# Delta heads of a hybrid decoder step: normalisation moved from keys and queries to factors per token

## The reference, cut to what matters

```
qkv_a  = h @ w_in[...];  conv = causal depthwise convolution of width 4 of q, k, v;  silu
qa = l2_normalize(qa) * HEAD_DIM_A ** -0.5
ka = l2_normalize(ka)              # x * rsqrt(sum(x*x) + 1e-6)
G = cumsum(log_a);  decay[i,j] = exp(G_i - G_j), i >= j
a_mat = strict lower part of (beta_i k_i . k_j) * decay
solve (I + a_mat) [w, u] = [beta k exp(G), beta v]
v_new = u - w S;   o = (q exp(G)) S + ((q . k) * decay) v_new
S = S * exp(G_last) + (k exp(G_last - G))^T v_new
o_a = rms_norm(o, gnorm_a) * silu(z)
```

## Time and profile before

| | us |
|---|---|
| median of 3 runs | 1989.44 (1988.54 to 1991.89) |
| the profiled execution's own time | 1989.23 |
| its span | 1987.2 |
| PE busy | 1910.3 (96% of the span) |
| DVE busy | 755.8 (38%) |
| ACT busy | 619.8 (31%) |
| POOL busy | 559.3 (28%) |

### The profile page before, as it was taken

The page is one execution under the profiler, slowest core; times in us unless marked ns, Lnnn a source line. Parts: engine busy times, 40 slices in busy tenths (PEclk is TensorE's granted clock), DMA queues, the critical chain, the costliest instruction groups (busy, mean ns, idle before and its releaser), DMA issues.

```text
span 1987.2 us, 29633 instructions
## 1 busy us (share of the span) xinstructions
PE 1910.3 (96%) x12298; PEld 1855.4 (93%) x12298; DVE 755.8 (38%) x1525; ACT 619.8 (31%) x1335; POOL 559.3 (28%) x332
## 2 busy tenths in 40 slices
PE   6899999999999999999989999999999999999998
PEld 6898998999999899988989999999999999999997
DVE  5552552552452312332346424641252145115413
ACT  5532342342342323334424323321231023103311
POOL 1241141131131110211114434531343234214431
PEclk9999999989999999999989999999999999999999
DMA  5312312312312432444554332221121122112212
GB/s 155 87 52 62 98 51 59 102 46 64 94 53 86 143 105 94 148 132 145 181 171 146 98 87 75 84 65 43 53 90 49 43 66 84 43 53 74 64 53 88
DMA packets 235839, 173.25 MB, mean 87 GB/s; under 512 B 16277, under 2 KB 225250, under 8 KB 235322
## 3 DMA queue, kind: packets, MB, share of 16 engines
q1 hardware_dynamic: 200586, 131.57, 22.4%
q10 hardware_dynamic: 35120, 39.80, 6.1%
HBM read 134.04 MB, written 47.72 MB: 91 GB/s over the span
## 4 chain that ended last, share of the span: by engine, by line
PE 81%; DVE 8%; ACT 4%; DMA 4%; issue 2%; POOL 1%; SPq 0%; DVEq 0%; ACTq 0%; POOLq 0%
PE dense L207 50%; PE dense L232 13%; PE work L1359 1%; PE work L1371 1%; PE work L995 1%; PE work L1005 1%; DVE systems L853 1%; PE work L1409 1%; PE work L207 1%; PE work L1392 1%; PE work L1351 1%; PE work L935 1%; PE work L1003 1%; PE work L962 1%; PE work L410 1%
## 5 line engine op out<-in xcount | busy, mean ns | idle before, releaser
L196 POOL TENSOR_TENSOR WL<-Wraw,WH 128x1024 fp32r<-128x1024 f32 (+1 forms) x131 | 315.3, 2407 | 1075.2 <-ACT WH L191 1075.1
L207 PE MATMUL dense<-hH,WH 128*128 128x352 f32 x1392 | 456.0, 328 | 5.5 <-POOL WL L196 5.5
L207 PE MATMUL dense<-hL,WH 128*128 128x352 f32 x1392 | 450.7, 324 | 0.0
L207 PE MATMUL dense<-hH,WL 128*128 128x352 f32 x1392 | 450.3, 324 | 0.0
L232 PE MATMUL dense<-hH,WH 128*128 128x352 f32 x744 | 268.8, 361 | 5.6 <-ACT fill L241 5.3
L207 PEld LDWEIGHTS dense<-hH,WH 128*128 128x128 f32 x1392 | 265.0, 190 | 6.9 <-POOL WL L196 5.7
L207 PEld LDWEIGHTS dense<-hL,WH 128*128 128x128 f32 x1392 | 265.1, 190 | 0.0
L207 PEld LDWEIGHTS dense<-hH,WL 128*128 128x128 f32 x1392 | 264.6, 190 | 0.0
L207 PE MATMUL dense<-gH,WH 128*128 128x352 f32 x768 | 247.5, 322 | 2.5 <-DVE gL L1754 1.7
L191 ACT ACTIVATE WH<-Wraw 128x1024 fp32r<-128x1024 f32 (+1 forms) x131 | 136.3, 1041 | 363.7 <-PE dense L207 296.3
L207 PE MATMUL dense<-gL,WH 128*128 128x352 f32 x768 | 247.8, 323 | 0.0
(11 more groups left out here) (318 smaller groups left out, 2652.0 us busy)
## 6 DMA issues: line engine op xcount, KB each, us to landing
Wraw<-in_w_in SPq DMA_DIRECT2D x51, 512.0 KB, 4.2
Wraw<-in_w_up SPq DMA_DIRECT2D x32, 512.0 KB, 4.0
Wraw<-in_w_down SPq DMA_DIRECT2D x32, 512.0 KB, 3.6
cache<-in_cache_win SPq DMA_DIRECT2D x20, 512.0 KB, 6.3
qkv_scratch<-fill ACTq DMA_DIRECT2D x54, 176.0 KB, 1.8
raw<-qkv_scratch SPq DMA_DIRECT2D x6, 1584.0 KB, 9.2
out_win_s<-in_cache_win ACTq DMA_DIRECT2D x16, 512.0 KB, 4.1
gb_scratch<-fill ACTq DMA_DIRECT2D x24, 176.0 KB, 2.5
```

What stands on the lines that cost most here:

```text
L196: G.tensor_tensor(WL[:, s, 0:k], Wraw[:, s, 0:k], WH[:, s, 0:k].bitcast(F32), ALU.subtract).then_inc(sem("w_split"), 1)
L207: ins = PE.matmul(out[:, 0:TN], w[:, s, k0 + k, :], x[:, k, cols], start=(k == 0 and i == 0), stop=(k == nk - 1 and i == 2))
```

## The change

k and q are used as they come from silu. With |k|^2 the sum of squares (plus 1e-6) and 1/|k|^2 called `rk2`: v is scaled with |k| beta (`cvb`), `at` and v_new with rk2, and q's norm and its constant go into the eps of the output's norm (`qeps`), which divides them out. So k's products are taken directly from silu(k) and silu(q), k and v are turned in one batch each, q is not turned, nothing is turned back, and only q's sum of squares is made by PE; ACT sums k's squares from the turned k. q with its decay is `qg`: Exp of cum on ACT, a product on POOL.

The order changes on every engine. PE turns k after 16 of v's 24 parts and makes k's products behind v's projection; 17 parts of z are followed by the tails, then v is turned. The fills lie elsewhere: 44 ahead of the T transposes, two in each gap of the levels, four or five per step of the scan. DVE makes the decays' subtractions between q's and k's convolution (in the first head behind k's) and v's convolution only when `at` is made. SP loads cum before the jobs 4 and 5, and loads 6 and 7 later.

The diff, cut:

```diff
+            for j in range(2, 4):
                 load(j)
             sp.wait_ge(sem("oa_stored"), 16 * h + 1)
             sp.wait_ge(sem("rows_out"), 32)
             sp.dma_start(cum_b[:], rows_d[bass.ds(h, 1), :].to_broadcast([P, T])).then_inc(sem("cum_loaded"), 16)
             sp.wait_ge(sem("at_made"), h + 1)
             sp.dma_start(beta_b[:], rows_d[bass.ds(h + 12, 1), :].to_broadcast([P, T])).then_inc(sem("beta_loaded"), 16)
+            for j in range(4, 6):
+                load(j)
...
+            load(6)
...
+            load(7)
...
+            split(2)
+            if h == 0:
+                split(3)
+                split(4)
...
+            pool.wait_ge(sem("silu"), 3 * h + 1)
+            G.tensor_tensor(qg[:], qg[:], qkv[:, 0], ALU.mult).then_inc(sem("emb_made"), 1)
+            if h:
+                split(3)
+                split(4)
+            pool.wait_ge(sem("at_made"), h + 2)
+            pool.wait_ge(sem("sq_q"), h + 1)
+            pool.wait_ge(sem("emb_made"), 3 * h + 3)
+            def lvl(s):
+                G.tensor_tensor(at_lvl[s], at[:, 0:NCH], masks[:, 2 + s:3 + s].to_broadcast([P, NCH, P]), ALU.mult).then_inc(sem("lvl_made"), 1)
+            lvl(0)
+            lvl(1)
+            split(5)
+            pool.wait_ge(sem("v_turned"), 3 * h + 3)
+            lvl(2)
...
+            def exps():
+                act.wait_ge(sem("e_arg"), h + 1)
+                A.activation(qg[:], cum_b[:], ACT.Exp)
+                A.activation(e_all[:, 0:NCH], e_all[:, 0:NCH], ACT.Exp)
+                A.activation(e_all[0:TS, NCH, 0:TS], e_all[0:TS, NCH, 0:TS], ACT.Exp).then_inc(sem("e_ready"), 1)
...
+            if h:
+                for t in range(NG):
+                    q_out(act, h, 0, t)
+            split(2)
+            q_out(act, h, 1, 0)
+            q_out(act, h, 1, 1)
+            if h:
+                exps()
+            q_out(act, h, 1, 2)
+            split(3)
+            silu(act, h, 0)
+            if h == 0:
+                ab_rows_out(act)
+            else:
+                act.wait_ge(sem("ss_done"), h)
...
+            q_out(act, h, 2, 0)
+            silu(act, h, 1)
+            q_out(act, h, 2, 1)
+            if h == 0:
+                ab_exps(act)
+                exps()
...
+            for i, lo, hi in ((1, 4, 8), (0, 0, 4), (2, 8, 9)):
+                if i == 1:
+                    act.wait_ge(sem("k_turned"), 3 * h + 2)
+                else:
+                    act.wait_ge(sem("ev_v"), 3 * h + i + 1)
+                for t in range(lo, hi):
+                    n = tokens[t][1]
+                    ins = A.activation(sqj[0:n, t], work[2 + i][0:n, P * (t - lo):P * (t - lo) + P], ACT.Square, accum_out=ssk[0:n, t:t + 1])
+                ins.then_inc(sem("squared"), 1)
+            q_out(act, h, 2, 2)
+            split(4)
+            act.wait_ge(sem("mean"), NT9 + 2 * h + 1)
+            A.activation(nk[:], ssk[:], ACT.Sqrt).then_inc(sem("root"), 1)
...
+            for i, (lo, hi) in enumerate(((0, 4), (4, 8), (8, 9))):
+                act.wait_ge(sem("v_turned"), 3 * h + i + 1)
+                for t in range(lo, hi):
+                    n = tokens[t][1]
+                    o = P * (t - lo) if i < 2 else P
+                    ins = A.activation(vb[0:n, t], work[(0, 1, 4)[i]][0:n, o:o + P], ACT.Copy, scale=cvb[0:n, t:t + 1])
+                ins.then_inc(sem("ev_a"), 1)
+            filled(0, 1, 2)
...
+            def decays():
+                dve.wait_ge(sem("cum_loaded"), 16 * h + 16)
+                dve.wait_ge(sem("cols_read"), 1)
+                chV.link(dve, V.tensor_copy(ccum[:], col[:, :, bass.ds(h, 1)].rearrange("p t o -> p (t o)")))
+                chV.link(dve, V.tensor_copy(cb[:], col[:, :, bass.ds(h + 36, 1)].rearrange("p t o -> p (t o)")))
+                for t, (c, n) in enumerate(tokens):
+                    ins = V.tensor_scalar(e_all[0:n, t, 0:n], cum_b[0:n, c:c + n], ccum[0:n, t:t + 1], 0.0, ALU.subtract, ALU.min)
+                ins.then_inc(sem("e_arg"), 1)
...
+            conv_of(0)
+            if h:
+                decays()
+            else:
+                ab_rows(dve)
+            conv_of(1)
+            if h == 0:
+                ab_cols(dve)
+                decays()
+            for i, (lo, hi) in enumerate(((0, 4), (4, 8))):
+                dve.wait_ge(sem("k_turned"), 3 * h + i + 1)
...
...
+            dve.wait_ge(sem("em_made"), 2 * h + 2)
+            for i in (0, 1, 4, 2, 3):
+                dve.wait_ge(sem("kk_done"), 5 * h + (0, 1, 3, 4, 2)[i] + 1)
+                if i < 4:
+                    V.tensor_tensor(qk_t[:, 2 * i:2 * i + 2], kk_of(i, 0), em[:, 2 * i:2 * i + 2], ALU.mult)
+                else:
+                    V.tensor_tensor(qk_t[0:TS, NCH, 0:TS], kk_of(i, 0), em[0:TS, NCH, 0:TS], ALU.mult)
+            dve.wait_ge(sem("squared"), 3 * h + 3)
+            V.tensor_scalar(ssk[:], ssk[:], EPS, None, ALU.add).then_inc(sem("mean"), 1)
+            dve.wait_ge(sem("mean"), NT9 + 2 * h + 1)
+            chV.link(dve, V.reciprocal(rk2[:], ssk[:]))
+            dve.wait_ge(sem("emb_made"), 3 * h + 2)
+            for t, (c, n) in enumerate(tokens):
+                x = kk_of(t // 2, 1)[:, t % 2] if t < NCH else kk_of(4, 1)
+                ins = V.scalar_tensor_tensor(out=at[0:n, t, 0:n], in0=x, scalar=rk2[0:n, t:t + 1], in1=emb[0:n, t, 0:n], op0=ALU.mult, op1=ALU.mult)
+            ins.then_inc(sem("at_made"), 1)
...
+            conv_of(2)
+            dve.wait_ge(sem("root"), NT9 + 2 * h + 1)
+            V.tensor_tensor(cvb[:], nk[:], cb[:], ALU.mult).then_inc(sem("cols_made"), 1)
...
-            V.tensor_scalar(osum[:], osum[:], 1.0 / HD, EPS, ALU.mult, ALU.add).then_inc(sem("mean"), 1)
+            V.scalar_tensor_tensor(out=osum[:], in0=osum[:], scalar=1.0 / HD, in1=qeps[:], op0=ALU.mult, op1=ALU.add).then_inc(sem("mean"), 1)
...
+            if h:
+                proj(0, 8, 24)
...
+            proj(1, 0, 24)
+            proj(2, 0, 8)
+            if h == 0:
+                ab_tensor(pe)
+            proj(2, 8, 16)
+            pe.wait_ge(sem("silu"), 3 * h + 2)
+            pe.wait_ge(sem("oa_part"), 3 * h + 1)
+            for i, (lo, hi) in enumerate(((0, 4), (4, 8), (8, 9))):
+                for t in range(lo, hi):
+                    c, n = tokens[t]
+                    ins = PE.transpose(work[2 + i][0:n, P * (t - lo):P * (t - lo) + P], qkv[:, 1, c:c + n], ident[:, :])
+                ins.then_inc(sem("k_turned"), 1)
+            proj(2, 16, 24)
+            if h == 0:
+                pe.wait_ge(sem("cols_read"), 1)
+            for i in (0, 1, 4, 2, 3):
+                if i == 4:
+                    pe.wait_ge(sem("ev_v"), 3 * h + 3)
+                    pe.wait_ge(sem("squared"), 3 * h + 3)
+                for t in ((2 * i, 2 * i + 1) if i < 4 else (NCH,)):
+                    c, n = tokens[t]
+                    o = 2 * P * (t % 2) if i < 4 else 256
+                    ins = PE.matmul(work[i][0:n, o:o + 2 * n].rearrange("p (x i) -> p x i", x=2), qkv[:, 1, c:c + n], qkv[:, 0:2, c:c + n], start=True, stop=True)
+                ins.then_inc(sem("kk_done"), 1)
+            proj(3, 0, 17)
             pe.wait_ge(sem("conv_done"), 3 * h + 3)
-            pe.wait_ge(sem("oa_part"), 3 * h + 1)
+            pe.wait_ge(sem("at_made"), h + 2)
             for j in range(3):
                 ins = PE.transpose(work[2][0:27, P * j:P * j + P], tails[:, j], ident[:, :])
             ins.then_inc(sem("tails_turned"), 1)
-            pe.wait_ge(sem("squared"), 2 * h + 2)
-            for x in range(2):
-                for t in range(NT9):
-                    ins = PE.matmul(work[4][:, NT9 * x + t:NT9 * x + t + 1], sq[:, x, P * t:P * t + P], ones[:, 0:1], start=True, stop=True)
+            proj(3, 17, 21)
+            pe.wait_ge(sem("silu"), 3 * h + 3)
+            for i, (lo, hi) in enumerate(((0, 4), (4, 8), (8, 9))):
+                for t in range(lo, hi):
+                    c, n = tokens[t]
+                    o = P * (t - lo) if i < 2 else P
+                    ins = PE.transpose(work[(0, 1, 4)[i]][0:n, o:o + P], qkv[:, 2, c:c + n], ident[:, :])
+                ins.then_inc(sem("v_turned"), 1)
+            proj(3, 21, 24)
+            fill_parts(0, 8)
+            pe.wait_ge(sem("sq_q"), h + 1)
+            pe.wait_ge(sem("ev_a"), 3 * h + 3)
+            for t in range(NT9):
+                ins = PE.matmul(work[4][:, t:t + 1], sqq[:, P * t:P * t + P], ones[:, 0:1], start=True, stop=True)
             ins.then_inc(sem("ss_done"), 1)
-            fill_parts(8, 15)
-            pe.wait_ge(sem("silu"), 3 * h + 3)
+            fill_parts(8, 20)
...
+            scanned = (60, 65, 69, 74, 78, 83, 87, 92)
```

More of the change, by code:

```diff
@@ L602, in split @@
                 split_lo(pool, N_HEAD + j, N_HEAD + j + 8 * h)
-            for j in range(2, 6):
-                split(j)
+            split(2)
+            if h == 0:
+                split(3)
+                split(4)
```

(41 more changed lines are left out.)

243 lines of the change are left out of this document (65 added, 178 removed).

## The result

The changed kernel takes 2017.54 us (median of 4 runs, 2012.04 to 2019.99) against 1988.99 for the kernel before beside it: ratio 1.0139, 95% interval 1.0114 to 1.0163. It is slower, as forecast (2015). The profiled execution took 2018.17 us, its span is 2016.2.

The account below looks back on a forecast made before the run. PE, busy 96% of the span, was taken to bound the kernel. New waits with their half clock, 63.4 us, against gains of 37.2 gave +26.2 on 1989.2: 2015 us, own range 2004 to 2025, overall 1979 to 2030.

Parts of the forecast that it names:

- wait at the first head's products: First head: PE reaches its fifth product at 87.4, its inputs kbg and kd at 88.7; waits 1.3 us.
- lost by clock: Half clock after each new PE wait, about 1.5 us each, less 2.3 saved in the third head; +8.2 us.
- work taken off PE: Per head 36 transposes (4.3 us) and half the column sums (2.0) go: 6.3 a head, 25.2 in all.
- Rival A: DVE's convolutions are not held up, as POOL's operations fall elsewhere or DVE gets through: 1981 us; chance 0.20.
- rival B: One block per convolution: k's held by emb alone (1.0), v's by one level product (2.4): 1998 us; chance 0.18.
- rival C: DVE gets no turn between POOL's queued operations; k's convolution starts after qg's product and the splits: 2030 us; chance 0.12.
- The first wait: PE, ready to turn k, waits for silu(k): 7.4 us in heads two to four, 0.5 in the first.
- taking turns: k's convolution on DVE alternates with POOL's em, emb and mask operations, standing 3.8 us in all.
- The second wait: PE, after 17 z parts, waits for v's convolution: 5.0 us in later heads, 9.5 or 13.9 in the first.
- the sum by that page: If plain copies on DVE also stand beside POOL, v's two add about 0.5 us a head: 2017 us.
- The waits for L978, L984 and L1077: PE's old waits at the small inverse (4.0), T transposes (2.6) and back transposes (3.1) go: 9.7 us.
- S + 14.0: Second head: when DVE has made `at`, counted in us from S, the end of silu(k) at 240.3.

Follow-up runs that it names:

- e1: Changed kernel with one more wait: POOL's chain of em, emb, mask, q's product and two splits starts after k's convolution; 1995.79 us.
- e2: Changed kernel with one more wait: POOL's level products start only when v's convolution is done; 1998.23 us.
- e3: Changed kernel with only q's product with the decay and what follows it on POOL waiting for k's convolution; 1997.93 us.
- e8: Kernel before, with q's 18 column sums moved ahead between the fourth and fifth fill part, k's left in place; 1983.33 us.
- e9: Changed kernel with both e1's and e2's aims, reordered splits, k turned behind all v parts, q's product and a split after v's convolution; 1959.88 us.
- e10: e9 with parts of z (12 in the first head, 3 in others) moved between k's fourth and fifth tile products; 1956.73 us.

## Why the prediction was right, point by point

All in us over the four heads, predicted and measured; the measured rest is what idle time and clock leave of the 27.9.

| term | predicted | measured |
|---|---|---|
| wait for silu(k) | 22.7 | 34.3 |
| wait for v's convolution | 28.9 | 27.8 |
| wait at the first head's products | 1.3 | not listed |
| PE's idle time in all, less what went | +43.2 | +51.5 |
| lost by clock | +8.2 | +5.8 |
| work taken off PE | -25.2 | -29.4 |
| sum | +26.2 | +27.9 |

**Where and why: as forecast.** Two waits at the places named, both behind DVE operations that POOL holds up. e1 and e2 take one each away and give 22 and 19 us back. Rival A, no hold-up, falls with the rows of 10.62 and 2.37; rival B, one block per convolution, with k's; rival C in the form that it had (k's convolution starts behind POOL's whole run) falls too, since one operation came through after the mask.

**The first wait was mis-sized**, 10.8 us a head where 7.4 stood. The step that failed is "taking turns", by which the hold-up was 3.8 us: 1.0 for the end of emb, 2.4 for the mask, the rest for short ones. Measured against e1, where the convolution runs free, it is 7.5. The decays and the mask make 3.0 of it: the mask 2.0, by which the three operations of e3 exceed 4.10, and em and emb 1.0 by way of the two copies, which cost no more because DVE waits 3.03 us for silu(q) behind them anyway, as e1's row shows. The other 4.5 are q's product and the split, which went in with no turn for DVE; e3 moves just these and gets 6.11 for the three operations and a wait of 6.1. So rival C was half right: POOL's next queued operation did go in ahead of a waiting one of DVE's, but not always. In the first head the wait was 2.0 instead of 0.5, and that is no hold-up, since POOL is idle there from 74.2 to 90.7: PE was ready at 79.2 instead of 80.0, and k's convolution ended at 79.9 instead of 79.2.

**The second wait was right in size, 4.9 against 5.0 and 13.2 against 13.9, by other operations.** The prediction let the convolution's own operations stand; in fact the short copies ahead of them did, 2.37 and 2.33 us for 0.17 and 0.18, which before's trace never showed beside POOL. That makes 4.35 of hold-up where 4.5 stood, on top of the 0.5 a head that e2 leaves. On these copies the Trainium skill, "SBUF — State Buffer", section "Who interferes with whom", was right where the sum was not: by it plain copies can take the shared port pair too, and here they stood. What the sum by that page would have added, 0.5 a head, does not show in the 4.9.

**Two gains and one loss were too small.** The first gain is the half clock behind the column sums. The prediction took half of the sums at their 4.08 us and never asked what the clock did behind them; in before it drops to 0.50 there (the rows at e8). In the changed kernel full clock follows the 18 that are left, and 10.2 us of loss are gone; e8 shows on the kernel before that parting the row does this. With them went 1.7 behind the third head's L978, where the prediction had put all of the 2.3 by which that head is longer, and 1.7 behind a wait of the first head (L552). The loss that was too small is that of the new half-clock stretches behind the two waits: 18.6 instead of 10.5. With 0.8 more at the start of the heads the net is +5.8.

The second gain is the work: every variant of the changed kernel has 537 to 539 us of it, before and its variants 566 to 568, a difference of 28 to 31 instead of 25.2. Where these 4 us are the runs do not show; the ends of matmuls are modelled, and the transposes and sums were priced from one stretch of the second head.

So 2015 against 2017.5 is partly luck: +11.6 on the first wait and about +8 on the new half-clock stretches stand against some 12 of clock and 4 of work that were not counted as gains. The waits for L978, L984 and L1077 went as said; the new 1.8 at L1119 was missed. Three sums of the prediction are off by 0.1 from their own terms (the 7.4, S + 14.0 and rival B's 4.4 should be 7.3, S + 14.1 and 4.5), which changes nothing.

**Which part of the change costs.** Less work on PE, the change's own subject, is worth 29 us, and the order that came with it costs more. e9 keeps the arithmetic; it adds two waits on POOL, moves two splits and q's product there, and eight parts on PE. Its idle time is 26.2 us, nearly before's 23.4, and its heads are 31 us shorter than before's.

## What to carry to other kernels

Before an elementwise chain is moved to POOL or earlier on it, lay its operations beside those of DVE that have all operands in SBUF and are on the path, the shortest ones too; here a wait that starts POOL's work behind them gave 22 and 19 us net, though the first of them made the next waits 8 us longer. When a PE wait is removed or shortened, look at the next wait of the same chain: where PE's work beside the chain is the same, as in e10, moving parts only moves the wait. And read the granted clock behind each group of instructions that a change removes or adds, such as the column sums here, not its own time alone; read it again in every variant, since behind the same 18 sums it stayed up in some and fell in others.

## What the runs showed of the hardware that was not expected

Operations on DVE of 3, 24 and 9 columns, which take 0.16 to 0.18 us alone, took 1.79 to 3.83 us beside POOL operations of 1024 and 1056 columns: a small operation stood as long as a large one, until POOL's running operation was over, and the one of 3.83 until two of POOL's were. It works the other way too: POOL's L621, 0.24 in the first head, took 1.29 behind a DVE operation. When both were waiting, POOL's next operation went first in some places (240.40 to 245.09 in the changed kernel) and DVE's in others (the first L816 operation, behind the mask at 239.19); what decides it these runs do not show.

A row of 36 one-column products on PE was followed by the lower clock four times out of four, for 3.2 to 6.5 us, with no idle time. Behind rows of 18 it came in 16 of the 36 heads of the changed kernel and its eight variants, and in none of e8's.
